# The arena ahead of the small tensors, and another order in the feed-forward prologue

## The reference

```
def swiglu(h, w_gate, w_up, w_down):
    return (jax.nn.silu(h @ w_gate) * (h @ w_up)) @ w_down
...
x = x + 0.5 * swiglu(rms_norm(x, ffn1_norm[l]), ffn1_w_gate[l], ffn1_w_up[l], ffn1_w_down[l])
x = x + hybrid_mixer(...)
x = x + memory_cross_attention(...)
x = x + 0.5 * swiglu(rms_norm(x, ffn2_norm[l]), ffn2_w_gate[l], ffn2_w_up[l], ffn2_w_down[l])
```

## Time and profile before

| | us |
|---|---|
| median of 3 runs | 2343.62 (2343.01 to 2344.78) |
| the profiled execution | 2343.6 |
| its span | 2341.8 |
| TensorE busy | 2309.2 |
| VectorE busy | 1815.4 |
| ScalarE busy | 1379.8 |
| DMA, share of 16 engines | 0.54 + 0.02 |
| mean granted TensorE clock | 0.996 of full speed |

### The profile page before, as it was taken

One profiled execution on the slowest core, in us unless ns is written; L12 is line 12 of the kernel. 1 busy time (PEld: TensorE's weight loads), 2 busy tenths in 40 slices (PEclk: granted clock), 3 DMA queues, 4 the chain that ended last, 5 costly groups with the idle time before them and its releaser, 6 DMA issues.

```text
span 2341.8 us, 33071 instructions
## 1 busy us (share of the span) xinstructions
PE 2309.2 (99%) x12395; PEld 1922.2 (82%) x12395; DVE 1815.4 (78%) x1974; ACT 1379.8 (59%) x1511; POOL 17.6 (1%) x15
## 2 busy tenths in 40 slices
PE   9999999999999999999999999999999999999999
PEld 7888889788878898887887888887887888888787
DVE  7887866788888877768888886477888888467887
ACT  6557456555666566655656654665656555564655
POOL 0000010000000001000000000000000000000000
PEclk9999999999999999999999999999999999999999
DMA  8656444565556554545565566546565656645553
GB/s 279 211 187 184 153 144 153 162 206 187 186 188 202 186 176 145 189 128 192 183 198 203 183 201 196 161 161 196 182 205 171 208 183 207 183 162 165 198 183 127
DMA packets 330999, 428.17 MB, mean 183 GB/s; under 512 B 17608, under 2 KB 296400, under 8 KB 330640
## 3 DMA queue, kind: packets, MB, share of 16 engines
q1 hardware_dynamic: 324832, 412.73, 54.1%
q10 hardware_dynamic: 6064, 13.98, 1.7%
HBM read 425.61 MB, written 1.05 MB: 182 GB/s over the span
## 4 chain that ended last, share of the span: by engine, by line
PE 96%; DVE 2%; issue 1%; ACT 1%; DMA 0%; ACTq 0%; DVEq 0%
PE ps L1358 15%; PE ps L1111 13%; PE ps L1223 13%; PE ps L1224 12%; PE ps L1228 12%; PE ps L1113 12%; PE ps L1112 12%; PE ps L1338 2%; PE ps L1124 1%; PE ps L1475 0%; DVE wlo L1842 0%; PE ps L1544 0%; PE ps L1554 0%; DMA xres<-in_x 0%; PE ps L1701 0%
## 5 line engine op out<-in xcount | busy, mean ns | idle before, releaser
L1842 DVE TENSOR_TENSOR wlo<-raw,whi 128x2048 fp32r<-128x2048 f32 x318 | 720.3, 2285 | 146.3 <-ACT whi L550 145.9
L550 ACT ACTIVATE whi<-raw 128x2048 fp32r<-128x2048 f32 x312 | 593.1, 1903 | 228.4 <-PE ps L1113 186.6
L1223 PE MATMUL ps<-whi,hT 128*128 128x512 f32 x1280 | 503.5, 393 | 0.0
L1224 PE MATMUL ps<-whi,hT 128*128 128x512 f32 x1280 | 499.9, 391 | 0.0
L1111 PE MATMUL ps<-whi,hT 128*128 128x512 f32 x856 | 343.4, 401 | 1.4 <-DVE hT L2420 1.1
L1228 PE MATMUL ps<-wlo,hT 128*128 128x512 f32 x1280 | 343.6, 390 | 0.0
L1113 PE MATMUL ps<-whi,hT 128*128 128x512 f32 x856 | 334.5, 391 | 0.0
L1112 PE MATMUL ps<-wlo,hT 128*128 128x512 f32 x856 | 333.8, 390 | 0.0
L1223 PEld LDWEIGHTS ps<-whi,hT 128*128 128x128 f32 x1280 | 240.1, 188 | 63.9 <-ACT prod L657 14.6
L1228 PEld LDWEIGHTS ps<-wlo,hT 128*128 128x128 f32 x1280 | 240.3, 188 | 50.5
L1224 PEld LDWEIGHTS ps<-whi,hT 128*128 128x128 f32 x1280 | 240.4, 188 | 48.9
(11 more groups left out here) (328 smaller groups left out, 3052.0 us busy)
## 6 DMA issues: line engine op xcount, KB each, us to landing
raw<-in_w_ffn SPq DMA_DIRECT2D x264, 512.0 KB, 4.5
raw<-in_w_in SPq DMA_DIRECT2D x144, 512.0 KB, 4.8
raw<-in_ffn_w_down SPq DMA_DIRECT2D x88, 512.0 KB, 4.2
raw<-in_ffn_w_up SPq DMA_DIRECT2D x86, 512.0 KB, 4.6
raw<-in_ffn_w_gate SPq DMA_DIRECT2D x86, 512.0 KB, 5.6
raw<-in_w_out SPq DMA_DIRECT2D x32, 512.0 KB, 4.3
gain<-in_gains ACTq DMA_DIRECT2D x16, 512.0 KB
raw<-in_cross_wk SPq DMA_DIRECT2D x16, 512.0 KB, 4.0
```

The lines of the kernel that those rows point to most:

```text
L550: act.activation(whi[:, s, :, 0:cols], raw[:, s, :, 0:cols], ACT.Copy).then_inc(hi_ready, units)
L1223: pe.matmul(ps[:, bank, :], hT_hi[:, t, k0 + k, :], whi[:, s, k, :], start=first and k == 0, stop=False, skip_group_check=True)
L1224: pe.matmul(ps[:, bank, :], hT_lo[:, t, k0 + k, :], whi[:, s, k, :], start=False, stop=False, skip_group_check=True)
L1842: dve.tensor_tensor(wlo[:, s, :, 0:cols], raw[:, s, :, 0:cols], whi[:, s, :, 0:cols].bitcast(F32), ALU.subtract).then_inc(lo_ready, units)
```

## The change

It moves the arena's allocation ahead of the small tensors. It cuts the 21 down matmuls into 8, 7 and 6. In the prologue ScalarE does `take_parts(0)` and `parts_hi(0)` right behind `block_hi(0, 0)`, then `first_evac(1)`, `block_hi(1, 0)`, `second_silu(1)`, `block_hi(2, 0)`, a split, `take_parts(1)` and a split. VectorE does `parts_sums(0)` right behind `block_lo(0, 0)`, puts `parts_lo(0)` behind the first of the three block sums, then both products, `block_lo(1, 0)`, `block_lo(2, 0)`, the splits, and only then `final_scale` or `joint_gain` where they are due. TensorE's wait for `up_out` ahead of `blocks(0, 0)` goes.

```diff
-CHUNKS = (0, 9, 16, 21)
+CHUNKS = (0, 8, 15, 21)
...
         cst = sb("cst", [P, N_CONST])
+        with nc.sbuf_tensor("rounded", [P, 18432], F32R) as rounded:
+            pass
+        arena = sb("arena", [P, 18432])
         stat = sb("stat", [P, 2, 3, TB])
...
         hinv = sb("hinv", [P, TB])
-        with nc.sbuf_tensor("rounded", [P, 18432], F32R) as rounded:
-            pass
-        arena = sb("arena", [P, 18432])
...
                 first_silu(off + 1)
                 block_hi(0, 0)
+                take_parts(0, bank=ACC + 1)
+                parts_hi(0)
                 if b == l == e == 0:
...
-                block_hi(1, 0)
-                take_parts(0, bank=ACC + 1)
                 act.wait_ge(half_inverse, f + 1)
                 first_evac(1, bank=TR + 1)
+                block_hi(1, 0)
+                second_silu(1)
                 block_hi(2, 0)
-                parts_hi(0)
                 split_hi(b, l, off + 5)
-                second_silu(1)
+                take_parts(1)
                 split_hi(b, l, off + 6, units=2)
-                take_parts(1)
                 block_hi(0, 1)
...
                 gate_up(1, 1)
-                pe.wait_ge(up_out, WIDE * f + 1)
                 blocks(0, 0, first=True)
...
-                def block_sums(j, c=0):
+                def block_sums(j, c=0, between=None):
...
+                    if between is not None:
+                        between()
                     dve.wait_ge(block_summed, 3 * n + 1)
...
                 block_lo(0, 0)
-                block_sums(0)
+                parts_sums(0)
+                block_sums(0, between=lambda: parts_lo(0))
+                kept_product(1)
+                bank_product(1)
+                block_lo(1, 0)
+                block_lo(2, 0)
+                split_lo(b, l, off + 5)
+                split_lo(b, l, off + 6, units=2)
                 if (b, l, e) == (1, 0, 0):
                     final_scale()
...
-                block_lo(1, 0)
-                parts_sums(0)
-                kept_product(1)
-                block_lo(2, 0)
-                parts_lo(0)
-                bank_product(1)
-                split_lo(b, l, off + 5)
-                split_lo(b, l, off + 6, units=2)
```

## The result

| | before | after |
|---|---|---|
| median of the runs, us | 2344.2 (2343.01 to 2346.06) | 2310.2 (2309.28 to 2310.48) |
| ratio, with 95% interval | | 0.9854 (0.9837 to 0.9871) |
| profiled execution, us | 2343.6 | 2310.08 |
| its span, us | 2341.8 | 2308.3 |
| mean granted clock | 0.996 | 0.999 |

The change takes 34 us off, 1.5%. The forecast was 2313.2 with 2309 to 2325 as its range: sign, size and place were right, and the kernel came out 3 us better than the single number.

The account below looks back on a forecast made before the run. TensorE, busy 99% of the span, was taken as the bound, leaving idle time, clock and matmul spacing to gain. Prologues 19.2, loop 1.4 and arena 9.8 took 30.4 us off 2343.6: 2313.2 us, range 2309 to 2325.

Parts of the forecast that it names:

- The ordinary prologue: Prologues of five of the eight feed-forwards: the 1.79 us TensorE wait and its restart go, 9.3 us together.
- The cover behind the product: Ordinary prologue: the product's last part is ready 1.3 us before TensorE reaches the down matmuls, so the wait goes.
- The small stall taken as 0.15: Ordinary prologue: late take_parts(1) and low halves for gate_up(2, 0) delay TensorE, 0.15 us for both.
- F3 and F4: Fourth and fifth feed-forwards' prologues: long waits and low clock go, short waits from moved VectorE work stay; 9.9 us saved.
- F0: First feed-forward's prologue: first wait goes, but seven DMA issues delay later work; 0, between a gain and loss of 2.
- The loop: 72 loop steps: smaller chunks start tile 0's gate_up one matmul earlier, saving 0.02 us each, 1.4 us.
- The arena: Loop steps and down matmuls: moving the arena to a multiple of 128 shortens mixed-operand matmul spacing, 9.8 us.
- The sum: Whole kernel: prologues 19.2, loop 1.4 and arena 9.8 give 30.4 us off 2343.6, so 2313.2 us.
- Rival 1: Arena: its address is not the cause and its move brings nothing; 2323.0 us, chance 0.25.
- Rival 2: Prologue steps 1 and 2: VectorE's late parts_lo(1) waits about 1 us in all eight feed-forwards; 2321 us, chance 0.10.
- Rival 3: Every loop step: turn_act waits for a late bank_product, making the kernel slower, 2350 us at 1.2 us slip; chance 0.03.
- Rival 4: Prologues: waits only move from blocks(0, 0) to step 2, leaving the loop's 1.4 us; 2342 us, chance 0.03.

Follow-up runs that it names:

- e4_order_only: The kernel before with only the new prologue order, old chunks and old arena place: 2324.49 us, ratio 0.9917.
- e11_scales: The changed kernel with final_scale and joint_gain moved out of the fifth and fourth feed-forwards' prologues into VectorE's idle stretches: 2307.82 us, ratio 0.9844.
- e10: The changed kernel with 128 unused bytes ahead of the arena, which stays in front of the small tensors: 2313.32 us.
- e2: The changed kernel with the arena back behind the small tensors, order and chunks as changed: 2321.34 us, ratio 0.9903.
- e9: The changed kernel with the arena back behind the small tensors and 96 unused bytes ahead of it: 2309.99 us.
- e7: The changed kernel with 32 unused bytes ahead of the first tensor, so the arena and the other operands all move: 2310.53 us.
- e3_chunks_only: The kernel before with only the chunks of 8, 7 and 6: 2341.79 us, ratio 0.9988.

## Why the prediction was right, point by point

**The ordinary prologue** (1.86 us each, F1, F2, F5, F6, F7). e4_order_only saves 1.77 to 2.07. The cover behind the product was counted at 1.3 us and is 1.4. The small stall taken as 0.15 is there: the weight load waits for L667 eight times, 2.8 us in total, and on TensorE the first matmul of `gate_up(2, 0)` keeps 461.91 - 461.58 = 0.33 us in F1 where its neighbours keep 0.23. Right.

```profile
461.58 0.50 PE L1223 MATMUL ps<-whi,hT 128*128 128x512 f32 x1
461.91 0.39 PE L1224 MATMUL ps<-whi,hT 128*128 128x512 f32 x1
```

**F3 and F4** (5.2 and 4.7). 5.3 and 4.7. The waits that were to be left, 0.75 and 1.07 with restart, are these two rows of the kernel after:

```profile
1070.89 0.73 PE L1358 MATMUL ps<-whi,rounded 128*128 128x512 f32 x2 [0.49 <-DVE rounded L1992]
...
1253.25 0.74 PE L1358 MATMUL ps<-whi,rounded 128*128 128x512 f32 x2 [0.99 <-DVE rounded L1992]
```

Both feed-forwards are 0.8 and 1.3 us longer than their neighbours, and e11_scales takes just that away. No low clock follows; in this window the kernel before had 0.74:

```profile
1062.00:1075.00 13.00, 12.51 (x58) 10.02 (x57) 12.77 (x15) 8.81 (x10) 0.00 (x0) 1.00 0.70 228
```

**F0** (0, within 2). The order is worth little there, as forecast (156.09 to 154.90 holds the arena's 1.3 and the chunks' 0.2, which leaves 0.3 of loss, inside a scatter of 1.9), and in part for the reason given: the DMA issues stand between `parts_hi(0)` and `first_evac(1)`. The step was too dear in its parts. The issues take from 30.09 to 33.45, 3.4 us and not 4.7, and `turn_act(1)` waits 0.83 (1.4 in e11_scales) and not 2.0. A wait that the sum had not listed stands in their place, 1.08 us at L1223 for `up_out` (L657), which was late behind the down weights (4.18 us of ScalarE's time, 4.25 in the earlier trace rows). The sum counted that row's wait among its reasons but gave it no price on TensorE.

**The loop** (1.4). Behind the new order the chunks are 0.2 a feed-forward, 1.8 in all; with the old order 0 to 0.17 a feed-forward. Right with the arena at its old place; what it missed is the tie to the next term.

**The arena** (9.8, of it 8.5 in the steps). 11.1 by the medians, 10.4 in the feed-forwards. The mechanism as a difference in spacing was right: chunk 0 went from 0.2333 to 0.2275. The term was undersized where it was guessed rather than read, in the matmuls of a step other than chunk 0. 10.4 / 72 = 0.144 us a step was gained and 0.118 counted; in settled steps it is 0.157. Chunk 0, now of eight matmuls, gives 0.045 of that, less than a third, where the sum had put it at half (0.06). Chunk 2 and the two `gate_up` give 0.113, where the sum had 0.05 to 0.06 for them. "A matmul that mixes an arena operand with one outside costs 0.0067 more" is therefore too narrow: 0.113 of 0.157 us is gained by matmuls that do not mix. The words used for it ("a multiple of 128") were wrong: e10 has that and is slower. That part is luck: the change happened to place the arena at a difference that is a multiple of 512, and e10 shows what a multiple of 128 alone would have brought.

**The sum.** Order 20.3 for 19.2, chunks 3.2 (or 1.8) for 1.4, arena 11.1 for 9.8. Of the 3 us by which the kernel is below the forecast, the arena's steps are 1.9 (10.4 for 8.5).

**The rivals.** Rival 1 (the address is not the cause, 2323) describes e2 within 2 us, but not the change. The rule it leaned on, in the Trainium skill, "TensorE: Matmul & The Clock Gate", section "Back-to-back issue gap", has the spacing hang on the columns and the clock, and in a stream of matmuls on the weight loads between them, which the prediction left out; here the same 512 columns with the same weight loads at a granted clock of 1.00 stood 0.2267 to 0.2333 us apart, depending on where the arena starts. The measurement decides. By the Trainium skill, "SBUF — State Buffer", section "Who interferes with whom", TensorE waits for no other engine's access. No run here shows another engine in its way, and none tests it; the spacing depends on the arena's start all the same. Rival 2 (a late `parts_lo(1)` in all eight) is seen in three, and in F0 for another reason. Rival 3 (`turn_act` in every step) would show at L1338, which waits once, in F0. Rival 4 falls with e4_order_only.

## What to carry to other kernels

Where an engine is dry once in a stage, look at what stands ahead of the one product it wants, on each queue that makes it; putting that chain first brought 20 us here, and whatever is moved behind it (DMA issues, occasional scaling) can turn up one step later; in F3 and F4 its size could be read from the rows of before (0.75 and 1.07 forecast, 0.8 and 1.3 measured), in F0 it could not. When matmuls of the same shape have two spacings in one trace, compare where their two operands lie before taking the slower one as given, and count the matmuls behind the slow group too. And give a stage's other waits one matmul of slack before making it faster, as otherwise they take part of the gain.

## What the runs showed of the hardware that was not expected

- The spacing of 128x512 fp32r matmuls at full granted clock was 0.2267 to 0.2333 us depending on where one tensor of operands started relative to the others. Differences of 32, 128, 416 and 448 (over a multiple of 512) were slower than 0, by 0.4 to 1.3 us for a feed-forward of 151.24. The place in memory (e9, 5632 bytes further on: 151.28) and a common offset of 32 bytes (e7: 151.29) had no effect. Over half of the loss, 0.090 of 0.157 us a step, fell on matmuls that use nothing of the tensor that was moved.
- Behind one and the same wait of 1.79 us in F5 the granted clock was 1.00 over the following 14 us in one execution and 0.79 over the following 7 us in another. Small gains elsewhere drown in that: the runs of e3_chunks_only span 6.3 us, and its 3.0 us of gain could not be put down to its edit.
